# Recurrent stage of a two-block kernel: product groups coupled in the array's quarters, and the key norm placed inside a dense tile

## The chip, the cores and the metric

The kernel runs on one core of one Trainium2 chip. The metric is the device time of one execution in microseconds. Before the change it is 2938.91 us (median of 3 runs, 2938.07 to 2939.73).

## What is computed

The reference applies two blocks to 1024 tokens of width 1024. The change lies in the second block's RWKV-7 branch: 8 heads of 64 channels, with a state matrix that is carried from token to token.

```python
w = jnp.exp(-DECAY_SCALE * jax.nn.sigmoid(w_logit))       # w_logit = w0 + tanh(wd) @ w_decay_up
a = jax.nn.sigmoid((a0 + ad @ w_iclr_up))
kk = k * k_k
kk = kk / jnp.maximum(jnp.linalg.norm(kk, axis=-1, keepdims=True), 1e-12)
k = k * (1.0 + (a - 1.0) * k_a)
...
def step(S, inp):
    r_t, w_t, k_t, v_t, kk_t, a_t = inp
    sa = jnp.einsum('bhvk,bhk->bhv', S, -kk_t)
    S = S * w_t[:, :, None, :] + sa[..., None] * (kk_t * a_t)[:, :, None, :] + v_t[..., None] * k_t[:, :, None, :]
    return S, jnp.einsum('bhvk,bhk->bhv', S, r_t)
```

The output is normed per head, gained, given the term sum(r k r_k) v, gated and multiplied by a matrix.

## The kernel before, in words

The stage handles two heads at a time (a *pair*, four in all; pairs 1 and 2 are a loop), one head on partitions 0 to 63 and one on 64 to 127. A pair takes its 1024 tokens in two *halves* of 512, and a half is eight chunks of 64 tokens. Inside a half the recurrence is solved by products of 64x64 matrices: a matrix `lt` is built, its inverse is approached in five *levels* (per level a product `t`, then `x` and `xt`), and at the end the state is carried through the eight chunks (`ms0` to `ms7`).

**Product groups.** One group is one product for two heads and eight chunks, 16 matmuls of 64x64 (each shows as two records, so x32). A matmul of that size occupies one quarter of TensorE's array. `SAME` writes a head to its own partitions and `OTHER` to the other head's, so a `SAME` group uses two quarters and an `OTHER` group the two that are left. Where the code issues one of each in turn, chunk by chunk, this text calls it a *couple*; before, `lt` with `lt_x`, `l` with `kkp_tm`, `ke_tm` with `akv`, and `x` with `xt` are such.

**Filling.** TensorE also has dense tiles to do (48 matmuls of 128x512, each tile in one of two PSUM pairs `dps[:, 0]` and `dps[:, 1]`). `fill(n)` in `rw_half_pe` issues the next n of them between the product groups (line 300, `dense_part`), so that TensorE has work while VectorE and ScalarE take the products out of PSUM. A *slot* is `fill(n - 1)`, the waits, `fill(1)` and a group or couple. Ahead of level 1 a slot has 2 dense matmuls, in the levels 5. What is left of a half's tiles follows at its end. At the end of every tile GpSimd splits the next tile's weights into `w_hi` and `w_lo` (lines 2376 and 2378).

**Banks.** Products rotate over three PSUM banks (`bank`, `BANKS = 3`); `free(name)` waits until the product three places earlier in `PRODUCTS.names` has been taken, by a mask on VectorE (`VALUES`) or a copy on ScalarE (`COPIES`). A fourth bank, `k.aps[:, 3, :]`, holds the half's output `y`, and between, the previous half's `mean` and `var`.

**Engines' queues.** The order of each engine is written out by hand and is counted in semaphores. VectorE: `rw_half_dve` masks the products in order (line 1891), subtracts `x` and `xt` (line 1915), and between them does one step each of two other lists: `result_step` (the previous half's output: `centred`, four reciprocals `rstd`, `normed`, `gained`, `summed` at line 1972, and the gating) and `setup_step` (the coming half's `l`, `lp`, `rate`, `floor`, four reciprocals `unit`, `kk`, `b`, `k`). A pair's first half has both lists (the first pair's first half has only the setup), its second half only the result.

**Opening of a pair.** `rw_pair_pe`: two products for decay and learning rate into `dps[:, 0]` and `dps[:, 1]` (line 1536), the key norm (line 1541; it needs `rw_e`, the squared key, from ScalarE at line 2005, and that needs VectorE's token shift of the key at line 1762), then a dense tile for `v` and one for a gate. ScalarE (`rw_pair_act`): square, scaled copy, sigmoid of the decay (line 2009), sigmoid of the rate (line 2012), root of the norm (line 2014), exponentials. VectorE (`rw_pair_dve`): shifts of key and `r`, the setup steps, the eight products ahead of the half (`rw_ahead_dve`, the last is `rkv`), then it takes `v` out of `dps[:, 0]` and shifts it, which the half's first step (line 1895) needs.

## Time and profile before

| | |
|---|---|
| median of 3 runs | 2938.91 us |
| profiled execution | 2935.31 us |
| its span | 2933.5 us |
| TensorE busy | 2758.5 us (94%) |
| VectorE, GpSimd, ScalarE busy | 1374.6, 945.1, 682.8 us |
| mean granted TensorE clock | 0.98 |
| the recurrent stage, four pairs | from 2008.8 to about 2706 us of the span |

A shortening of TensorE's queue counts where no other engine is late. The rows tell it by stretch: busy time of an engine against the stretch, the wait in brackets ahead of a row, and what ended it. Matmul records overlap (each starts before the one ahead has ended), so the cost of one in a row of them is the distance between starts.

### The profile page before, as it was taken

What the parts mean: (1) busy time and instruction counts of PE and PEld (TensorE: products, weight loads), DVE (VectorE), ACT (ScalarE), POOL (GpSimd) and SP (SyncE); (2) the same over time, 40 slices, a digit from 0 to 9 for tenths busy, and PEclk for the clock granted to TensorE, in tenths of its full rate; (3) what the DMA queues carried; (4) which work ended last, traced back from release to release, by engine and by line L of the source; (5) the groups of instructions that cost most, each with busy time, mean ns of one, the idle gap of its engine ahead of it and who ended that gap; (6) DMA issues with size and microseconds to landing.
All of it is one profiled execution on the core that took longest, in us unless ns stands there. A gap on an engine that the chain in (4) does not pass through costs nothing. (4 is left out here: it accounts for less than half of the span.)

```text
span 2933.5 us, 48563 instructions
## 1 busy us (share of the span) xinstructions
PE 2758.5 (94%) x20356; PEld 2195.1 (75%) x20356; DVE 1374.6 (47%) x1332; ACT 682.8 (23%) x966; POOL 945.1 (32%) x417
## 2 busy tenths in 40 slices
PE   7999999999999999999998989989999999998886
PEld 6777778887888888888876767776767767676675
DVE  7844441124532122212565643345457465564589
ACT  3433330011211001000233234441222121222321
POOL 4222214443444444444533211103111121213365
PEclk9999999999999999999999999999999999998998
DMA  3100001112111111111121100001011111112343
GB/s 124 36 29 29 29 15 50 50 44 107 43 50 49 45 50 50 46 47 50 57 79 65 65 22 14 14 29 59 31 42 34 49 38 42 34 42 95 115 151 107
DMA packets 40746, 156.11 MB, mean 53 GB/s; under 512 B 4640, under 2 KB 5152, under 8 KB 39200
## 3 DMA queue, kind: packets, MB, share of 16 engines
q1 hardware_dynamic: 31392, 110.21, 11.4%
q10 hardware_dynamic: 9216, 43.78, 4.0%
q8 instruction: 121, 1.98, 0.3%
q14 instruction: 17, 0.14, 0.0%
HBM read 133.00 MB, written 20.97 MB: 52 GB/s over the span
## 5 line engine op out<-in xcount | busy, mean ns | idle before, releaser
L2376 POOL TENSOR_TENSOR w_hi<-w_raw,one 128x1024 fp32r<-128x1024 f32 x199 | 389.8, 1959 | 1931.9 <-PE dps L283 1500.4
L283 PE MATMUL dps<-h_hi,w_hi 128*128 128x512 f32 x1904 | 608.3, 395 | 46.0 <-issue 11.1
L283 PE MATMUL dps<-h_lo,w_hi 128*128 128x512 f32 x1904 | 602.2, 392 | 0.0
L283 PE MATMUL dps<-h_hi,w_lo 128*128 128x512 f32 x1904 | 600.2, 391 | 0.0
L2378 POOL TENSOR_TENSOR w_lo<-w_raw,w_hi 128x1024 fp32r<-128x1024 f32 x199 | 527.5, 2651 | 15.6
L283 PEld LDWEIGHTS dps<-h_hi,w_hi 128*128 128x128 f32 x1904 | 358.4, 190 | 134.8 <-issue 40.3
L283 PEld LDWEIGHTS dps<-h_lo,w_hi 128*128 128x128 f32 x1904 | 360.8, 190 | 75.8 <-issue 0.2
L283 PEld LDWEIGHTS dps<-h_hi,w_lo 128*128 128x128 f32 x1904 | 360.5, 189 | 76.1
L300 PE MATMUL dps<-h_hi,w_hi 128*128 128x512 f32 x352 | 128.8, 426 | 5.3 <-DVE rw_t L1891 5.3
L300 PE MATMUL dps<-h_lo,w_hi 128*128 128x512 f32 x352 | 129.5, 430 | 2.5 <-DVE rw_t L1891 1.6
L300 PE MATMUL dps<-h_hi,w_lo 128*128 128x512 f32 x352 | 121.7, 412 | 1.6 <-DVE rw_t L1891 1.6
L932 DVE TENSOR_TENSOR tmp<-dps,inv 128x1024 f32<-128x1024 f32 x22 | 26.9, 1225 | 204.6 <-PE dps L283 204.6
L283 PE MATMUL dps<-hid_hi,w_hi 128*128 128x512 f32 x352 | 108.4, 389 | 0.0
L283 PE MATMUL dps<-hid_lo,w_hi 128*128 128x512 f32 x352 | 108.4, 389 | 0.0
L283 PE MATMUL dps<-hid_hi,w_lo 128*128 128x512 f32 x352 | 108.4, 389 | 0.0
L946 DVE TENSOR_TENSOR x_res<-dps,x_res 128x1024 f32 x24 | 29.4, 1225 | 156.1 <-PE dps L283 156.1
L957 ACT ACTIVATE tmp<-tmp 128x1024 f32<-128x1024 f32 x22 | 23.3, 1061 | 336.9 <-DVE tmp L930 336.9
L678 DVE TENSOR_TENSOR_SCAN sb_f<-sb_f,zero 128x128 f32<-128x128 f32 (+7 forms) x64 | 88.1, 1377 | 19.1 <-ACT sb_f L735 18.9
L1269 PE MATMUL aps<-mla_k,mla_q 128*128 128x512 f32 (+2 forms) x192 | 81.3, 534 | 13.7 <-ACT mla_p L1410 9.0
L300 PEld LDWEIGHTS dps<-h_lo,w_hi 128*128 128x128 f32 x352 | 64.8, 188 | 29.0 <-issue 4.4
L784 DVE TENSOR_TENSOR tmp<-dps,inv 128x1024 f32<-128x1024 f32 x16 | 19.6, 1225 | 140.7 <-PE dps L283 140.7
L300 PEld LDWEIGHTS dps<-h_hi,w_hi 128*128 128x128 f32 x352 | 63.6, 187 | 28.5 <-DVE rw_t L1891 10.0
(355 smaller groups left out, 4218.7 us busy)
## 6 DMA issues: line engine op xcount, KB each, us to landing
w_raw<-w_stream SPq DMA_DIRECT2D x200, 512.0 KB, 3.3
x_again<-x_t ACTq DMA_DIRECT2D x2, 4096.0 KB, 13.0
gates<-gate_out ACTq DMA_DIRECT2D x16, 512.0 KB, 2.9
tmp<-gates ACTq DMA_DIRECT2D x16, 512.0 KB, 4.3
x_t<-x_res ACTq DMA_DIRECT2D x4, 1024.0 KB, 3.9
out_t<-x_again SPq DMA_DIRECT2D x16, 256.0 KB, 2.0
back<-branches ACTq DMA_DIRECT2D x7, 512.0 KB, 8.9
x_res<-x_t ACTq DMA_DIRECT2D x2, 1536.0 KB, 12.1
```

The costliest lines, as they stand in the source:

```text
L283: mm = k.nc.tensor.matmul(k.dps[0:rows, pair, h * HALF:(h + 1) * HALF], w[:, slot, sub + t, 0:rows], x(t)[:, h * HALF:(h + 1) * HALF], sta ...
L300: mm = k.nc.tensor.matmul(k.dps[:, pair, h * HALF:(h + 1) * HALF], w[:, slot, t, :], x[:, t, h * HALF:(h + 1) * HALF], start=n < 2, stop=n ...
L678: v.tensor_tensor_scan(back, back, k.zero[:, 0:1].to_broadcast([P, w]), 1.0, ALU.mult, ALU.add).then_inc(k.sem("sb_scan_done"), 1)
L784: v.tensor_tensor(k.tmp[g][:, :], k.dps[:, g, :], k.inv[:, :], ALU.mult).then_inc(k.sem(f"pair{g}_out"), 1)
L932: v.tensor_tensor(k.tmp1[:, :], k.dps[:, 1, :], k.inv[:, :], ALU.mult).then_inc(k.sem("pair1_out"), 1)
L946: v.tensor_tensor(one(k.x, n), k.dps[:, j, :], one(k.x, n), ALU.add).then_inc(k.sem(f"pair{j}_out"), 1)
L957: a.activation(k.tmp0[:, :], k.tmp0[:, :], ACT.Silu).then_inc(k.sem("silu_done"), 1)
L1269: mm = mul(k.aps[:, 2 * r + lo // HALF, 0:hi - lo], k.mla_q[:, b * P:(b + 1) * P], k.mla_k[:, lo:hi], start=True, stop=False, skip_group_c ...
L2376: g.tensor_tensor(k.w_hi[:, s], k.w_raw[:, s], ones, ALU.mult).then_inc(k.sem("w_hi_done"), 1)
L2378: g.tensor_tensor(k.w_lo[:, s], k.w_raw[:, s], k.w_hi[:, s].bitcast(F32), ALU.subtract).then_inc(k.sem("w_split"), 1)
```

## The change

In the diff `each`, `mul` and `turn` issue the 16 matmuls of a group. Lines cut are marked.

```diff
@@ -1436,11 +1436,13 @@
 
-PRODUCTS = Steps("rw_product", ["rk", "lt", "lt_x", "l", "kkp_tm", "ak_t", "rb_t", "rk_t", "v_tm", "be_tm", "ke_tm", "akv"]
-                 + LEVEL_NAMES + ["u0", "w1", "n", "m", "r"] + [f"ms{c}" for c in range(NC)])
-VALUES = Steps("rw_value", ["rkv", "lt", "xt_part", "xt0", "x_part", "x0", "ak_t", "rb_t", "rk_t"] + LEVEL_NAMES
-               + ["decay", "m", "r", "s_in"] + [f"s{c}" for c in range(NC)])
-COPIES = Steps("rw_copy", ["kkp_tm", "v_tm", "be_tm", "ke_tm", "akv", "u0", "w1", "n"])
+BESIDE = {"t2": "rk_t", "t3": "be_tm", "t4": "ke_tm"}
+LEVEL_PRODUCTS = [n for name in LEVEL_NAMES for n in (name, BESIDE.get(name)) if n is not None]
+PRODUCTS = Steps("rw_product", ["rk", "lt", "lt_x", "l", "kkp_tm", "ak_t", "v_tm", "akv", "rb_t"]
+                 + LEVEL_PRODUCTS + ["u0", "w1", "n", "m", "r"] + [f"ms{c}" for c in range(NC)])
+VALUES = Steps("rw_value", ["rkv", "lt", "xt_part", "xt0", "x_part", "x0", "ak_t", "rb_t"]
+               + [n for n in LEVEL_PRODUCTS if not n.endswith("_tm")] + ["decay", "m", "r", "s_in"] + [f"s{c}" for c in range(NC)])
+COPIES = Steps("rw_copy", ["kkp_tm", "v_tm", "akv", "be_tm", "ke_tm", "u0", "w1", "n"])
 
@@ -1448,6 +1450,7 @@
             **{n: (VALUES, n) for n in ["ak_t", "rb_t", "rk_t"] + LEVEL_NAMES + ["m", "r"]}, **{n: (COPIES, n) for n in COPIES.names}}
+ROTATING = [n for n in PRODUCTS.names if n not in BESIDE.values()]
 
@@ -1481,7 +1484,7 @@
 def bank(k, name):
-    return k.aps[:, PRODUCTS.names.index(name) % BANKS, :]
+    return k.aps[:, ROTATING.index(name) % BANKS if name in ROTATING else BANKS, :]
 
@@ -1530,17 +1533,19 @@
     pe.wait_ge(k.sem("rw_up_loaded"), i * 16 + 16)
-    for n, (use, done) in enumerate(((use0, "rw_w_done"), (use1, "rw_a_done"))):
-        pe.wait_ge(k.sem(f"pair{n}_out"), use + 2)
-        for h in range(2):
-            mm = mul(k.dps[:, n, h * HALF:(h + 1) * HALF], k.rw_up[HEADS[n], :], k.rw_wdad[HEADS[n], h * HALF:(h + 1) * HALF],
-                     start=True, stop=True)
-        mm.then_inc(k.sem(done), 1)
+    pe.wait_ge(k.sem("pair0_out"), use0 + 2)
+    pe.wait_ge(k.sem("pair1_out"), use1 + 2)
+    for h in range(2):
+        w, a = (mul(k.dps[:, n, h * HALF:(h + 1) * HALF], k.rw_up[HEADS[n], :], k.rw_wdad[HEADS[n], h * HALF:(h + 1) * HALF],
+                    start=True, stop=True) for n in range(2))
+    w.then_inc(k.sem("rw_w_done"), 1)
+    a.then_inc(k.sem("rw_a_done"), 1)
+    dense_part(k, pe, blk + 2, 0, 0, use0 + 2, "blk_done", 0, 3 * KT)
     pe.wait_ge(k.sem("rw_kk_sq_done"), i + 1)
...
     mm.then_inc(k.sem("rw_kk_norm_done"), 1)
-    dense(k, pe, blk + 2, 0, 0, rows(k.h_hi), rows(k.h_lo), KT, 0, use0 + 2, "blk_done")
+    dense_part(k, pe, blk + 2, 0, 0, use0 + 2, "blk_done", 3 * KT, 6 * KT)
     dense(k, pe, blk + 3, 1, 0, rows(k.h_hi), rows(k.h_lo), KT, 1, use1 + 2, "blk_done")
@@ -1572,7 +1577,7 @@
 
-        u.wait(pe, *TAKEN_BY[PRODUCTS.names[PRODUCTS.names.index(name) - BANKS]])
+        u.wait(pe, *TAKEN_BY[ROTATING[ROTATING.index(name) - BANKS]])
 
@@ -1631,39 +1636,44 @@
     free("ak_t")
+    free("v_tm")
     fill(1)
     each("ak_t", SAME, channel("kq"), channel("kkp"))
-    fill(FILL_MASKS - 1)
-    free("rb_t")
-    free("rk_t")
-    fill(1)
-    each("rb_t", SAME, channel("bq"), channel("rp"))
-    each("rk_t", SAME, channel("kq"), channel("rp"))
+    for c in range(NC):
+        mm = turn(bank(k, "v_tm"), SAME, c, value)
+    mm.then_inc(product, 1)
     if before is not None:
...
     fill(FILL_MASKS - 1)
-    free("v_tm")
-    free("be_tm")
-    fill(1)
-    for name, lhs in (("v_tm", value), ("be_tm", chunk("be"))):
-        for c in range(NC):
-            mm = turn(bank(k, name), SAME, c, lhs)
-        mm.then_inc(product, 1)
-    fill(FILL_MASKS - 1)
-    free("ke_tm")
     free("akv")
+    free("rb_t")
+    u.wait(pe, COPIES, "v_tm")
     fill(1)
     for c in range(NC):
-        a = turn(bank(k, "ke_tm"), SAME, c, chunk("ke"))
-        b = mul(bank(k, "akv"), OTHER, c, same("akt"), same("v_tm"))
+        a = mul(bank(k, "akv"), OTHER, c, same("akt"), same("v_tm"))
+        b = mul(bank(k, "rb_t"), SAME, c, channel("bq"), channel("rp"))
     a.then_inc(product, 1)
...
     for l in LEVEL_STEPS:
+        beside = BESIDE.get(f"t{l}")
         fill(FILL_T - 1)
...
         u.wait(pe, VALUES, "x0" if l == 1 else f"x{l - 1}")
+        if beside == "rk_t":
+            if before is not None:
+                before.wait(pe, Y_COPIES, "std")
+        elif beside is not None:
+            u.wait(pe, *TAKEN_BY[BESIDE[f"t{l - 1}"]])
         fill(1)
-        each(f"t{l}", OTHER, same("lt"), same("xm"))
+        for c in range(NC):
+            a = mul(bank(k, f"t{l}"), OTHER, c, same("lt"), same("xm"))
+            if beside == "rk_t":
+                b = mul(bank(k, "rk_t"), SAME, c, channel("kq"), channel("rp"))
+            elif beside is not None:
+                b = turn(bank(k, beside), SAME, c, chunk(beside[0:2]))
+        a.then_inc(product, 1)
+        if beside is not None:
+            b.then_inc(product, 1)
         fill(FILL_X - 1)
@@ -1683,9 +1693,7 @@
     u.wait(pe, VALUES, f"xt{LEVELS}")
-    u.wait(pe, COPIES, "akv")
-    if before is not None:
-        before.wait(pe, Y_COPIES, "std")
+    u.wait(pe, COPIES, "ke_tm")
     fill(1)
@@ -1901,14 +1909,18 @@
     result_step()
-    for name, out, which in (("ak_t", "akt", "strict_t"), ("rb_t", "arbt", "incl_t"), ("rk_t", "arkt", "incl_t")):
+    for name, out, which in (("ak_t", "akt", "strict_t"), ("rb_t", "arbt", "incl_t")):
         u.wait(dve, PRODUCTS, name)
...
         mask("t1", f"t{l}", f"lev{l}").then_inc(made, 1)
-        result_step()
+        if BESIDE.get(f"t{l}") == "rk_t":
+            u.wait(dve, PRODUCTS, "rk_t")
+            mask("arkt", "rk_t", "incl_t").then_inc(made, 1)
+        else:
+            result_step()
         for n, out in (("x", "xm"), ("xt", "xt")):
@@ -1983,6 +1995,7 @@
     a.activation(k.rw_wdad[0:HD, :], k.rw_wdad[0:HD, :], ACT.Tanh).then_inc(k.sem("rw_tanh_done"), 1)
+    rw_up_load(k, act, 0, w_up)
     rw_pair_act(k, act, 0, None, w_up, branches, gates)
@@ -1996,10 +2009,13 @@
 
+def rw_up_load(k, act, i, w_up):
+    act.dma_start(k.rw_up[:, :], w_up[bass.ds(i, 1)].rearrange("a p n -> p (a n)")).then_inc(k.sem("rw_up_loaded"), 16)
 def rw_pair_act(k, act, i, before, w_up, branches, gates):
...
     use0, use1 = i * RW_USES + (RW_USE0 + 1), i * RW_USES + RW_USE1
-    act.dma_start(k.rw_up[:, :], w_up[bass.ds(i, 1)].rearrange("a p n -> p (a n)")).then_inc(k.sem("rw_up_loaded"), 16)
     act.wait_ge(k.sem("rw_mix_done"), i * 3 + 2)
@@ -2010,6 +2026,8 @@
     a.activation(k.rw_b[:, :], k.dps[:, 1, :], ACT.Sigmoid, bias=vec(k, "a0", i)).then_inc(k.sem("pair1_out"), 1)
+    if not isinstance(i, int) or i < PAIRS - 1:
+        rw_up_load(k, act, i + 1, w_up)
     act.wait_ge(k.sem("rw_kk_norm_done"), i + 1)
@@ -2075,18 +2093,19 @@
         rw_result_act(k, act, before, "std")
-    copy("be_tm")
-    copy("ke_tm")
     copy("akv")
     if after is None:
-        for n in (2, 3):
-            rw_gate_act(k, act, u, n, gates)
-        if end:
-            back_load(k, act, u, branches, gates)
+        rw_gate_act(k, act, u, 2, gates)
     else:
...
         rw_exps_act(k, act, after)
+    copy("be_tm")
+    copy("ke_tm")
+    if after is None:
+        rw_gate_act(k, act, u, 3, gates)
+        if end:
+            back_load(k, act, u, branches, gates)
     copy("u0", -1.0)
```

The new order of a half's products: `ak_t` and `v_tm` one after the other in one slot; `akv` coupled with `rb_t`; `rk_t` coupled with `t2`, `be_tm` with `t3`, `ke_tm` with `t4`. The last three write the fourth bank. Two slots fewer stand ahead of level 1.

**TensorE, opening of the first pair.** Before, with `rw_e` the squared key and line 1536 the products for decay and rate:

```order
L283 MATMUL dps<-h_hi,w_lo 128x512 x2
L1536 MATMUL dps<-rw_wdad,rw_up 128x512 x4
L1541 MATMUL aps<-rw_e,const 128x512 x2
L283 MATMUL dps<-h_hi,w_hi 128x512 x2
L283 MATMUL dps<-h_lo,w_hi 128x512 x2
```

and with the change:

```order
L283 MATMUL dps<-h_hi,w_lo 128x512 x2
L1539 MATMUL dps<-rw_wdad,rw_up 128x512 x4
L300 MATMUL dps<-h_hi,w_hi 128x512 x2
L300 MATMUL dps<-h_lo,w_hi 128x512 x2
...
L300 MATMUL dps<-h_hi,w_lo 128x512 x2
L1546 MATMUL aps<-rw_e,const 128x512 x2
L300 MATMUL dps<-h_hi,w_hi 128x512 x2
```

The norm now has 24 dense matmuls of the `v` tile ahead of it and 24 behind.

**TensorE, first half, ahead of level 1.** Before (`rw_kq` stands in `ak_t` and `rk_t`, `rw_v`, `rw_be`, `rw_ke` in the groups that turn them into `v_tm`, `be_tm`, `ke_tm`, `rw_akt` in `akv`):

```order
L1581 MATMUL aps<-rw_kkp_154,rw_kq_158 64x64 x16
L300 MATMUL dps<-h_hi,w_hi 128x512 x2
L1581 MATMUL aps<-rw_rp_152,rw_bq_156 64x64 x16
L1581 MATMUL aps<-rw_rp_152,rw_kq_158 64x64 x16
L300 MATMUL dps<-h_lo,w_hi 128x512 x2
L1587 MATMUL aps<-const,rw_v 64x64 x16
L1587 MATMUL aps<-const,rw_be_160 64x64 x16
L300 MATMUL dps<-h_hi,w_lo 128x512 x2
L1587 MATMUL aps<-const,rw_ke_162 64x64 x2
L1581 MATMUL aps<-rw_v_tm,rw_akt 64x64 x2
```

and with the change, to the start of the couple in level 2:

```order
L1586 MATMUL aps<-rw_kkp_154,rw_kq_158 64x64 x16
L1592 MATMUL aps<-const,rw_v 64x64 x16
L300 MATMUL dps<-h_hi,w_hi 128x512 x2
L1586 MATMUL aps<-rw_v_tm,rw_akt 64x64 x2
L1586 MATMUL aps<-rw_rp_152,rw_bq_156 64x64 x2
...
L300 MATMUL dps<-h_hi,w_hi 128x512
L1586 MATMUL aps<-rw_xm,rw_lt 64x64 x16
...
L1586 MATMUL aps<-rw_xm,rw_lt 64x64 x2
L1586 MATMUL aps<-rw_rp_152,rw_kq_158 64x64 x2
```

Four slots have become two; rows in turn of x2 are couples.

**VectorE, first half, from the masks ahead of level 1 into level 2**, with the change:

```order
L1899 TENSOR_TENSOR rw_akt<-aps,const 128x512
L1899 TENSOR_TENSOR rw_arbt<-aps,const 128x512
L1816 SCALAR_TENSOR_TENSOR rw_l<-const,rw_sg 128x512
L1899 TENSOR_TENSOR rw_t_170<-aps,const 128x512
...
L1899 TENSOR_TENSOR rw_t_170<-aps,const 128x512
L1899 TENSOR_TENSOR rw_arkt<-aps,const 128x512
L1927 TENSOR_TENSOR rw_xm<-rw_xm,aps 128x512
```

Before, the mask `rw_arkt` stood directly behind `rw_arbt`; it is now behind the mask of `t2`.

## Rows read from the trace of the kernel before

**Rows 1.** The page's first part: busy us and share of the span of each engine.

```profile
PE 2758.5 (94%) x20356; PEld 2195.1 (75%) x20356; DVE 1374.6 (47%) x1332; ACT 682.8 (23%) x966; POOL 945.1 (32%) x417
```

**Rows 2.** Busy time by stretch, pair 1; columns: stretch, its us, then PE, PEld, DVE, ACT, POOL, granted clock, DMA.

```profile
2193.30:2216.50 23.20, 23.20 (x97) 19.06 (x97) 20.14 (x22) 7.01 (x9) 4.62 (x2) 0.94 0.07 23
...
2216.50:2289.60 73.10, 70.42 (x1272) 52.91 (x1271) 40.81 (x64) 16.94 (x23) 13.64 (x6) 1.00 0.12 42
...
2289.60:2360.00 70.40, 70.00 (x1271) 52.67 (x1269) 29.89 (x46) 9.51 (x14) 13.14 (x6) 1.00 0.13 45
```

**Rows 3.** Timeline of PE, pair 0, first half; columns: start, us, engine, line, operation, count.

```profile
2039.71 0.62 PE L283 MATMUL dps<-h_hi,w_lo 128*128 128x512 f32 x2
...
2042.43 0.62 PE L283 MATMUL dps<-h_hi,w_lo 128*128 128x512 f32 x2
...
2047.82 0.73 PE L300 MATMUL dps<-h_hi,w_lo 128*128 128x512 f32 x2
...
2049.56 0.73 PE L300 MATMUL dps<-h_hi,w_hi 128*128 128x512 f32 x2
...
2052.23 0.73 PE L300 MATMUL dps<-h_lo,w_hi 128*128 128x512 f32 x2
...
2054.91 0.73 PE L300 MATMUL dps<-h_hi,w_lo 128*128 128x512 f32 x2
...
2056.66 0.73 PE L300 MATMUL dps<-h_hi,w_hi 128*128 128x512 f32 x2
```

**Rows 4.** Timeline of PE, ACT and DVE, opening of pair 1.

```profile
2189.88 3.78 PE L1541 MATMUL aps<-rw_e,const 128*128 128x512 f32 x4 [4.45 <-ACT rw_e L2005]
...
2192.18 1.11 ACT L2009 ACTIVATE rw_sg<-dps,vec 128x1024 f32<-128x1024 f32 x1
...
2193.35 1.22 PE L283 MATMUL dps<-h_hi,w_hi 128*128 128x512 f32 x2
...
2194.36 1.05 PE L283 MATMUL dps<-h_lo,w_hi 128*128 128x512 f32 x2
...
2195.22 1.03 PE L283 MATMUL dps<-h_hi,w_lo 128*128 128x512 f32 x2
...
2195.62 1.03 ACT L2014 ACTIVATE rw_norm<-aps 128x1024 f32<-128x1024 f32 x1
...
2196.68 0.43 DVE L1817 TENSOR_SCALAR rw_norm<-rw_norm 128x512 f32<-128x512 f32 x1 [1.00 <-ACT rw_norm L2014]
...
2211.04 0.74 DVE L1863 SCALAR_TENSOR_TENSOR rw_rkv<-rw_r,vec,rw_k 128x512 f32<-128x512 f32 x1
...
2214.32 1.29 DVE L1762 SCALAR_TENSOR_TENSOR rw_v<-rw_d,vec,rw_v 128x1024 f32<-128x1024 f32 x1
```

**Rows 5.** Busy time by stretch: two restarts of PE (columns as in Rows 2).

```profile
2193.30:2196.10 2.80, 2.80 (x8) 2.17 (x8) 2.31 (x3) 2.77 (x3) 0.00 (x0) 0.50 0.00 0
...
1618.40:1622.60 4.20, 4.15 (x10) 3.31 (x11) 2.45 (x2) 1.65 (x2) 0.00 (x0) 0.50 0.00 0
```

**Rows 6.** Timeline of POOL and DVE, shift of the key, pair 1.

```profile
2184.25 3.20 POOL L2378 TENSOR_TENSOR w_lo<-w_raw,w_hi 128x1024 fp32r<-128x1024 f32 x1
...
2185.41 3.12 DVE L1762 SCALAR_TENSOR_TENSOR rw_k<-rw_d,vec,rw_k 128x1024 f32<-128x1024 f32 x1 [0.16 <-DVE rw_d L1760]
```

**Rows 7.** Timeline of DVE (pair 0) and of PE (pair 1), start of a half.

```profile
2048.00 0.68 DVE L1891 TENSOR_TENSOR rw_xm<-aps,const 128x512 f32<-128x512 f32 x1
...
2220.54 0.27 PE L1581 MATMUL aps<-rw_bq,rw_kkp 64*64 64x64 f32 x2
```

**Rows 8.** Timeline of POOL, DVE and PE, level 4 and 5.

```profile
2144.34 1.89 POOL L2376 TENSOR_TENSOR w_hi<-w_raw,one 128x1024 fp32r<-128x1024 f32 x1 [28.01 <-PE dps L300]
...
2144.42 2.36 DVE L1972 TENSOR_TENSOR rw_centred<-rw_centred,rw_rkv 128x512 f32<-128x512 f32 x1
...
2251.42 1.47 DVE L1972 TENSOR_TENSOR rw_centred<-rw_centred,rw_rkv 128x512 f32<-128x512 f32 x1
...
2258.05 0.49 PE L300 MATMUL dps<-h_hi,w_hi 128*128 128x512 f32 x1 [1.25 <-DVE rw_t L1891]
```

## The prediction

> **What bounds the kernel now.** I read the page first: TensorE is busy for 94% of the span [rows 1], so what shortens TensorE's own queue shortens the kernel, unless an engine that it waits for is late. Then the busy time by stage [rows 2]. The second half of a pair is TensorE alone (70.0 us busy of 70.4); the first half is 73.1 us long with 70.4 busy, so 2.7 us of it are waits, and the reader should see that VectorE is busy there for 40.8 us against 29.9. Then TensorE's timeline in a half, for the price of a product group [rows 3], and the timeline of a pair's opening, for the chain ahead of the half [rows 4]. There TensorE waits 4.45 us for the squared key, does the key norm in 3.5 us, and goes straight into the dense tile at 2193.35, which I call S below.
>
> **The product groups.** From the dense matmuls ahead of the `ak_t` slot to those ahead of `t1` it is 2056.66 - 2047.82 = 8.84 us [rows 3]: four slots with six group times and eight dense matmuls. The change leaves two slots. One holds two groups one after the other (`ak_t`, `v_tm`), as the slot from 2049.56 to 2052.23 does now: 2.67 us. One holds a couple (`akv` with `rb_t`), as the slot from 2054.91 to 2056.66: 1.75 us. `rk_t`, `be_tm` and `ke_tm` ride in `t2`, `t3`, `t4`; a couple there costs what a single group costs, since the `kq` group alone (2047.82 to 2049.56, 1.74 us with its two dense matmuls) is as long as the couple's slot. The four dense matmuls left out are done at the end of the half, 0.91 us at 0.227 each (twelve from 2039.71 to 2042.43). Sum: 8.84 - 2.67 - 1.75 - 0.91 = 3.51 saved in a half, **28.1 us** in eight. Bounds: no less than 2 x 0.93 us (2.67 - 1.74, a group time for each of `rk_t` and `be_tm`), and 4.42 where a half has no dense work to fill with (the very last).
>
> One new wait stands inside: `v_tm` takes the bank of `l`, so the `ak_t` slot now waits for the mask of `l`. That mask ran to 2048.68 [rows 7], while the second dense matmul of the slot started at about 2048.15. The wait costs about 0.45 us in each half, **+3.6 us**. Behind it are queued the rest of the slot and everything after it. `akv` now waits for the copy of `v_tm` soon after its product; the `var` product and one dense matmul cover that, except in the first half of all, which has no `var` product (half a us, in the range). The copies of `be_tm` and `ke_tm` move behind the exponentials or a gate copy on ScalarE; nothing needs them before levels 4 and 5, and ScalarE is busy for 17 of 73 us [rows 2], so I cost them at nothing. In level 2 the mask of `rk_t` (0.69 us) takes the place of one step of the result; cost nothing by itself.
>
> **The opening: TensorE's part.** The dense tile writes the bank that the decay product was in, so it starts when ScalarE's first sigmoid is done: 2192.18 + 1.11 = 2193.29, and the dense start is 2193.35 [rows 4]. The norm product ended at that same moment. The change does not touch ScalarE's order (square, scaled copy, sigmoid), so the tile cannot start earlier; taking the norm out of the wait frees nothing, and it costs its own time inside the tile. At the high clock its four passes take half of the 0.85 us that they take now, 1.7 us, with 0.1 around them: 1.8 us. Second, the wait is now empty: TensorE stands still for some 8 us before S, where the norm had half woken it. At S the granted clock is the low one (0.5) until 2196.10 today [rows 5]; after that it is the high one. From its first matmul at 2189.88 that is 6.2 us. At another restart, at 1618.4, it was low for 4.2 us. I take 5.1 us from S, between the two. A dense matmul takes 0.43 us at low clock (2194.36 to 2195.22 for two [rows 4]) and 0.227 at high, so each us at low clock loses 0.47. Against the 1.9 to 2.75 us at low clock that lie behind S today it is 2.7 us more on average: +1.25 us. A pair: 1.8 + 1.25 = 3.05, four pairs **+12.2 us**. Bounds for the clock part: 0.7 us (4.2) to 1.8 us (6.2) a pair. The decay and learning-rate products are interleaved; they end in front of the same wait, so they are worth nothing either way. The load of `rw_up` is issued from another place of ScalarE's queue, where it has time in hand.
>
> **The opening: VectorE's part.** The norm now ends after 24 dense matmuls, S + 5.1 + 12.4 x 0.227 + 1.8 = S + 9.7. With the root (1.03 us) and the hand-overs VectorE takes `floor` at S + 10.95 instead of S + 3.33 (2196.68) [rows 4]: 7.6 us later. From there it is 15.1 us of its own work to the end of `rkv` at 2211.78, so S + 26.05, and I add 0.35 because more of it now falls beside GpSimd: S + 26.4. TensorE is ready for the `rk` product at S + 26.0. So far nothing is lost. But VectorE then takes `v` and shifts it, and the `rkv` of the half and the mask of `lt` queue behind that. Today `v` is ready at 2215.61, 0.9 us before `rk` at 2216.5. In the new order the take begins just as the second tile ends, and that is when GpSimd splits the next weights. What this does stands at the shift of `k`, in the same position [rows 6]: its second operation took 3.12 us and ended 1.1 us after GpSimd's, where that of `v` today, with GpSimd idle, takes 1.29 [rows 4]; the operation ahead of it was lengthened as well. I take the dear values: `v` is ready at S + 32.4, the mask of `lt` ends at S + 33.8, the `l` group starts at S + 34.3. TensorE alone would be there at today's S + 27.2 [rows 7] + 3.0 = S + 30.2. Loss 4.1 us a pair, **+16.4 us**. Bounds: the cheap values take 2.0 us off a pair; a low clock of 4.2 or 6.2 us moves it by 0.4.
>
> **The levels.** A half now has eight dense matmuls before level 1 and ten in a level, so the 48th, which ends a tile and lets GpSimd split weights, moves from before the `x4` slot into it. GpSimd then works from about 0.25 to 4.7 us after the slot's start, and VectorE's next operation on two SBUF inputs starts some 2.4 us after it: `summed` where a result is computed, `kk` in the first half of all. Such an operation waited for GpSimd's to end and ended 0.55 us behind it: `summed` took 2.36 us beside a split of 1.89, and 1.47 where the meeting was shorter [rows 8]. It would now end 5.25 us after the slot's start, with the mask of `t5` behind it, and in first halves a reciprocal and `kk` as well. Against the waits of today (1.25 us at that mask in a first half, part of the 2.7 [rows 2, 8]) I get 2.1 us more in the three first halves that carry both, 1.3 in the very first, 0.6 in second halves: 6.3 + 1.3 + 2.4 = **+10.0 us**. Bounds: nothing (the meeting falls elsewhere) to 15.
>
> **Sum.** -28.1 + 3.6 + 12.2 + 16.4 + 10.0 = +14.1 us, against the profiled execution of 2935.3 us: 2949.4. The median of the runs shown is 3.6 us above that execution, so 2953.0 us. A measurement of this kernel can tell 0.2% (5.9 us) from no change: below 2933.0 is faster, above 2944.8 slower.
>
> **The rivals.** (a) *VectorE catches up* (faster, 0.14): the key norm's delay is absorbed, the `l` group starts when TensorE gets there and the levels meet no split. Then only TensorE's own terms count: -28.1 + 3.6 + 12.2 = -12.3, so 2926.6. For it: VectorE is idle for 3 us of the 23 behind S [rows 2]. Against: `v` has only 0.9 us in hand and gets 7.6 us of delay less the 3 that TensorE loses too. It decides where the `v` shift ends: before S + 28.
>
> (b) *Half of the meetings with GpSimd do not happen* (no change, 0.18): cheap shift (-8.0) or cheap levels (-10.0), or both: +6 to -4, 2935 to 2945.
>
> (c) *The products leave PSUM too slowly* (slower, 0.04): rows 2 show VectorE busy for 40.8 of 73.1 us in a first half, and more products now come at once. If the extra mask in level 2 held up every half by its 0.69 us, that is 5.5 more: 2958.5. The Trainium skill, TensorEngine Tiling (Array Packing), Performance Considerations, says that tiling speeds up TensorE but not the evacuation of PSUM, which can then be the bottleneck. By that rule the couples would be worth less than their slots; the rows bear it out in first halves only.
>
> (d) *The couples do not overlap* (slower, 0.04): each of the three new couples in a level costs a second group, about 1.0 us: 3 x 8 = 24 more, 2977. Against it stand the equal slots of rows 3.
>
> **How the numbers follow.** The forecast itself has 0.60: 2946 to 2963, from the clock's bounds (4 us either way over four pairs) and the levels' (5 up). With (c) and (d) slower has 0.68, (b) gives same 0.18, (a) faster 0.14. The range for 8 in 10 leaves out (a) and (d) and takes in (b): 2934 to 2963.
>
> **What would show it.** Right: `t2` to `t4` slots no longer than today; the dense tile's start still on the first sigmoid; VectorE's `v` shift at over 4 us beside a split; the granted clock low for 4 to 6 us behind each dense start; second halves near 68 us (70.4 - 3.5 + 0.45 + 0.6), first halves near 76 (73.1 + 4.1 - 3.5 + 0.45 + 2.1). Wrong: the `l` group starting without a wait, or first halves that shrink as the second ones do; then (a) holds. A dense start before the sigmoid's end would overturn the opening's whole term.

## The result, and the profile after

The changed kernel takes 2957.03 us (median of 4 runs, 2956.03 to 2957.95), the kernel before 2938.49 (4 runs, 2937.75 to 2939.73). The ratio is 1.0059, with a 95% interval of 1.0044 to 1.0075: slower by 18.5 us. The profiled execution took 2957.55 us, its span is 2955.8, its mean granted clock 0.974.

The page's first part, the counterpart of [rows 1]. TensorE is busy for 18 us less than before, in a span that is 22 us longer; the change did take work out of TensorE's queue, and waits grew by more.

```profile
PE 2740.1 (93%) x20356; PEld 2182.3 (74%) x20356; DVE 1381.6 (47%) x1332; ACT 685.1 (23%) x966; POOL 946.5 (32%) x417
```

Busy time by stretch of pair 1, columns as in [rows 2]: from the dense start to the half, the first half, the second half.

```profile
2201.97:2228.71 26.74, 26.36 (x101) 20.60 (x101) 17.03 (x20) 6.96 (x9) 4.86 (x3) 0.90 0.06 20
...
2228.70:2305.80 77.10, 69.36 (x1271) 51.57 (x1272) 46.69 (x67) 17.27 (x23) 13.46 (x6) 0.98 0.11 40
...
2305.80:2373.60 67.80, 66.40 (x1271) 50.05 (x1269) 29.27 (x46) 9.83 (x14) 12.82 (x6) 1.00 0.13 45
```

The second half went from 70.4 to 67.8 us, the first from 73.1 to 77.1, although TensorE is busy for 1.1 us less in it; the stretch ahead went from 23.2 to 26.7. The waits of TensorE name the engines (columns: who waited for what, us in total, times, longest).

```profile
PE dps L300 <- ACT rw_sg L2025: 31.3, 4, 7.9
PE dps L300 <- DVE rw_t L1899: 16.0, 16, 2.6
PE dps L300 <- DVE rw_lt L1899: 14.0, 4, 4.1
```

The wait for the first sigmoid is the old standstill in front of the norm, which the norm no longer interrupts. The one for the mask of `lt` is new, and that for the masks of `t` was 8.6 us before, 15 times.

The opening of pair 1 in the timeline of PE, ACT, DVE and POOL; it answers to [rows 4, 6].

```profile
2200.80 1.11 ACT L2025 ACTIVATE rw_sg<-dps,vec 128x1024 f32<-128x1024 f32 x1
...
2201.97 1.22 PE L300 MATMUL dps<-h_hi,w_hi 128*128 128x512 f32 x2 [7.90 <-ACT rw_sg L2025]
...
2210.08 1.88 PE L1546 MATMUL aps<-rw_e,const 128*128 128x512 f32 x4
2211.39 1.03 PE L300 MATMUL dps<-h_hi,w_hi 128*128 128x512 f32 x2
...
2213.05 0.43 DVE L1825 TENSOR_SCALAR rw_norm<-rw_norm 128x512 f32<-128x512 f32 x1 [8.75 <-ACT rw_norm L2032]
...
2227.91 0.75 DVE L1871 SCALAR_TENSOR_TENSOR rw_rkv<-rw_r,vec,rw_k 128x512 f32<-128x512 f32 x1
2228.57 1.22 DVE L1780 TENSOR_TENSOR rw_v<-dps,inv 128x1024 f32<-128x1024 f32 x1
2229.82 1.66 DVE L1768 TENSOR_TENSOR rw_d<-rw_v 128x1024 f32<-128x1024 f32 x1
2231.63 3.15 DVE L1770 SCALAR_TENSOR_TENSOR rw_v<-rw_d,vec,rw_v 128x1024 f32<-128x1024 f32 x1
...
2228.47 1.93 POOL L2395 TENSOR_TENSOR w_hi<-w_raw,one 128x1024 fp32r<-128x1024 f32 x1 [6.25 <-PE dps L283]
2230.48 3.21 POOL L2397 TENSOR_TENSOR w_lo<-w_raw,w_hi 128x1024 fp32r<-128x1024 f32 x1
...
2236.26 0.50 PE L300 MATMUL dps<-h_lo,w_hi 128*128 128x512 f32 x1 [3.31 <-DVE rw_lt L1899]
2236.69 0.28 PE L1586 MATMUL aps<-rw_bq,rw_kkp 64*64 64x64 f32 x2
```

The reader should see three things. The dense tile starts 0.06 us behind the end of the first sigmoid, as before. VectorE stands still for 8.75 us until the root of the norm is there. Its chain then reaches `v` 0.1 us after GpSimd's first operation has begun, the last operation of the shift takes 3.15 us where 1.29 was enough before [rows 4], and the `l` group starts at S + 34.72.

Level 5 of the same half, timeline of DVE, POOL and PE: `summed` (line 1984) takes 2.64 us beside the split, and the dense matmul that follows the mask of `t5` waits for 2.55 us.

```profile
2264.72 1.89 POOL L2395 TENSOR_TENSOR w_hi<-w_raw,one 128x1024 fp32r<-128x1024 f32 x1 [31.02 <-PE dps L300]
2266.69 2.37 POOL L2397 TENSOR_TENSOR w_lo<-w_raw,w_hi 128x1024 fp32r<-128x1024 f32 x1
...
2266.96 2.64 DVE L1984 TENSOR_TENSOR rw_centred<-rw_centred,rw_rkv 128x512 f32<-128x512 f32 x1
...
2271.85 0.50 PE L300 MATMUL dps<-h_lo,w_hi 128*128 128x512 f32 x1 [2.55 <-DVE rw_t L1899]
```

And what the prediction did not have. Stretches behind standstills (columns as in [rows 2], the last but two is the granted clock): behind the dense start; from the `l` group to `t1` in the first halves of pairs 0, 1, 2 and 3; and behind the level-5 wait.

```profile
2201.97:2207.40 5.43, 5.43 (x13) 4.32 (x14) 2.29 (x3) 2.23 (x2) 0.00 (x0) 0.50 0.00 0
...
2056.04:2066.91 10.87, 10.65 (x202) 8.22 (x201) 3.75 (x6) 1.79 (x3) 0.00 (x0) 0.63 0.11 44
2236.69:2245.03 8.34, 7.99 (x204) 5.91 (x204) 4.67 (x8) 4.93 (x7) 0.00 (x0) 1.00 0.18 67
2418.75:2428.18 9.43, 9.39 (x205) 6.86 (x204) 4.66 (x8) 4.94 (x7) 0.00 (x0) 0.82 0.16 59
2602.36:2613.38 11.02, 10.89 (x204) 8.00 (x203) 4.60 (x8) 4.30 (x6) 0.00 (x0) 0.69 0.13 50
...
2272.25:2275.66 3.41, 3.41 (x37) 2.98 (x37) 1.50 (x4) 0.00 (x0) 0.00 (x0) 0.50 0.00 0
```

Behind most of the new waits inside a half TensorE's clock is at its lower level (0.50, which is 1.2 GHz) for a while. The same slots take 8.34 us at the full clock and 9.43 to 11.02 where part of them runs at the low one.

**The stage in a sum.** With the starts of the same matmuls in the timeline as marks (tile end, dense start, `rk`, `l`, `t1`, `u0`), and sums over the four pairs:

| stretch | before | after | difference |
|---|---|---|---|
| start of the stage | 2008.7 | 2009.8 | +1.1 |
| dense start to `rk` | 91.8 | 105.2 | +13.5 |
| `rk` to `l`, first halves | 15.9 | 32.3 | +16.3 |
| `l` to `t1`, first halves | 47.7 | 39.7 | -8.0 |
| `l` to `t1`, second halves | 48.6 | 33.5 | -15.1 |
| `t1` to `u0`, first halves | 109.6 | 118.9 | +9.3 |
| `t1` to `u0`, second halves (three) | 76.3 | 77.8 | +1.5 |
| `u0` to the end of a half (seven) | 200.7 | 207.5 | +6.8 |
| last `t1` to the end of the stage | 45.8 | 45.6 | -0.2 |
| behind the stage | 226.8 | 223.9 | -2.9 |

The tile end to the dense start (11.36 us a pair) and `rk` to `l` of second halves (4.03) are the same in both.

### The profile page after: what moved, and what is told of

It reads as the page before. It is cut to its first block and busy times, and to the rows that moved or that the text cites. A ratio compares the mean times of both kernels' runs of the same rounds, so it can differ in the third digit from the quotient of the medians.

```text
span 2955.8 us, 48554 instructions
## 1 busy us (share of the span) xinstructions
PE 2740.1 (93%) x20356; PEld 2182.3 (74%) x20356; DVE 1381.6 (47%) x1332; ACT 685.1 (23%) x966; POOL 946.5 (32%) x417
## 5 line engine op out<-in xcount | busy, mean ns | idle before, releaser
L283 PE MATMUL dps<-h_hi,w_lo 128*128 128x512 f32 x1840 | 580.7, 391 | 0.0
L2397 POOL TENSOR_TENSOR w_lo<-w_raw,w_hi 128x1024 fp32r<-128x1024 f32 x199 | 531.2, 2669 | 15.6
L283 PEld LDWEIGHTS dps<-h_hi,w_lo 128*128 128x128 f32 x1840 | 348.0, 189 | 73.0
L300 PE MATMUL dps<-h_hi,w_lo 128*128 128x512 f32 x416 | 151.6, 428 | 4.2 <-DVE rw_t L1899 2.0
L932 DVE TENSOR_TENSOR tmp<-dps,inv 128x1024 f32<-128x1024 f32 x22 | 26.9, 1225 | 204.6 <-PE dps L283 204.6
L300 PEld LDWEIGHTS dps<-h_hi,w_lo 128*128 128x128 f32 x416 | 80.0, 195 | 30.7 <-DVE rw_xm L1899 5.2
```

Source lines behind the costliest of these rows:

```text
L283: mm = k.nc.tensor.matmul(k.dps[0:rows, pair, h * HALF:(h + 1) * HALF], w[:, slot, sub + t, 0:rows], x(t)[:, h * HALF:(h + 1) * HALF], sta ...
L300: mm = k.nc.tensor.matmul(k.dps[:, pair, h * HALF:(h + 1) * HALF], w[:, slot, t, :], x[:, t, h * HALF:(h + 1) * HALF], start=n < 2, stop=n ...
L932: v.tensor_tensor(k.tmp1[:, :], k.dps[:, 1, :], k.inv[:, :], ALU.mult).then_inc(k.sem("pair1_out"), 1)
L2397: g.tensor_tensor(k.w_lo[:, s], k.w_raw[:, s], k.w_hi[:, s].bitcast(F32), ALU.subtract).then_inc(k.sem("w_split"), 1)
```

## The experiments

The first theory in the texts below is the prediction's: fewer slots shorten TensorE's queue, but the later norm carries VectorE's `v` shift into GpSimd's split. Ratios are to the kernel before in the same job, whose median was 2939.2 us for the first four kernels and 2937.6 for the others.

### The groups without the opening

```diff
-    dense_part(k, pe, blk + 2, 0, 0, use0 + 2, "blk_done", 0, 3 * KT)
...
-    dense_part(k, pe, blk + 2, 0, 0, use0 + 2, "blk_done", 3 * KT, 6 * KT)
+    dense(k, pe, blk + 2, 0, 0, rows(k.h_hi), rows(k.h_lo), KT, 0, use0 + 2, "blk_done")
```

The products for decay and rate stand one after the other again, as before.

> The changed kernel with the pair's opening put back (products for decay and rate one after the other, the key norm ahead of the dense tile). Theory 1 (the opening costs about 30 us: 13.5 in TensorE's own queue and 16 in the wait for VectorE at the l group; the groups are a gain, given back in part by VectorE meeting GpSimd in the levels): 2926 us, 12 us under the kernel before; second halves 2.2 us shorter than before, first halves of pairs 1 to 3 about as long as before. Theory 2 (products cannot be taken from PSUM fast enough, the groups are the loss): 2938 or more. Theory 3 (the opening costs only TensorE's own 12 us, the rest of the loss lies in the groups): 2945.

Measured: 2919.88 us (6 runs), ratio 0.9938 (0.9926 to 0.9951): 19.4 us faster than before, 37 faster than the whole change. Its waits for the masks of `t`, for the mask of `l` (written to `rw_xm`), and for that of `lt`:

```profile
PE dps L300 <- DVE rw_t L1897: 15.3, 16, 2.6
PE dps L300 <- DVE rw_xm L1897: 3.2, 8, 0.5
...
PE dps L300 <- DVE rw_lt L1897: 0.4, 1, 0.4
```

The wait for `lt` is gone (0.4 us once, as before), that for the masks of `t` stays: the one belongs to the opening, the other to the groups. `l` to `t1` takes 33.3 us in the four first halves, against 47.7 before and 39.7 with the whole change; without the `lt` wait there is no low clock there. The gain is above the expected one, and about 3 us of that lie behind the recurrent stage, where this kernel needs 223.6 us.

### The norm inside the tile, on the kernel before

```diff
+    dense_part(k, pe, blk + 2, 0, 0, use0 + 2, "blk_done", 0, 3 * KT)
     pe.wait_ge(k.sem("rw_kk_sq_done"), i + 1)
...
-    dense(k, pe, blk + 2, 0, 0, rows(k.h_hi), rows(k.h_lo), KT, 0, use0 + 2, "blk_done")
+    dense_part(k, pe, blk + 2, 0, 0, use0 + 2, "blk_done", 3 * KT, 6 * KT)
```

> The kernel before with one edit: the key norm issued after the first 24 dense matmuls of the v tile. Theory 1: 30 us above the kernel before, 2968; the stretch from the dense start to the rk product 3.3 us longer in each pair and from there to the l group 4.0 us longer. Theory 3: 12 to 13 us above, 2951, with nothing between rk and l. Theory 2: 18 us above at most, 2957.

Measured: 2981.59 us (4 runs), ratio 1.0146 (1.0131 to 1.0161): 42.4 us slower. The two terms that were foreseen measure +14.5 (dense start to `rk`) and +16.6 (`rk` to `l`), as in the whole change. The rest is 5.4 us of low clock behind the `lt` wait (the last stretch of this view) and 4.7 us behind the stage; the four make 41.2 us, and the spans differ by 40.5.

```profile
2202.51:2229.53 27.02, 26.64 (x100) 20.80 (x100) 17.02 (x20) 6.96 (x9) 4.85 (x3) 0.89 0.06 20
2237.81:2251.10 13.29, 13.29 (x301) 10.63 (x301) 5.74 (x8) 4.17 (x7) 0.00 (x0) 0.82 0.10 39
```

The parts alone sum to -19.4 + 42.4 = +23.0 us; together they give +18.5. So they hardly act on each other, and the opening alone makes the change slower.

### The norm after 6 dense matmuls instead of 24

```diff
-    dense_part(k, pe, blk + 2, 0, 0, use0 + 2, "blk_done", 0, 3 * KT)
+    dense_part(k, pe, blk + 2, 0, 0, use0 + 2, "blk_done", 0, 6)
...
-    dense_part(k, pe, blk + 2, 0, 0, use0 + 2, "blk_done", 3 * KT, 6 * KT)
+    dense_part(k, pe, blk + 2, 0, 0, use0 + 2, "blk_done", 6, 6 * KT)
```

> The changed kernel with the key norm after 6 dense matmuls of the tile and not after 24; TensorE's work is the same. Theory 1: the norm is ready some 5.5 us sooner, v is shifted before GpSimd begins to split, and the wait at the l group goes (4.0 us a pair) with the low clock that follows it: 2932 us. Theory 3 (only TensorE's own time counts): unchanged, 2957. If VectorE's lateness counts but not GpSimd: the wait shrinks to nothing as well, so this run tells theory 1 from 3 and not GpSimd's part.

Measured: 2934.51 us (12 runs), ratio 0.9987 (0.9978 to 0.9995): 22.5 us below the changed kernel. In the timeline of pair 1 the last operation of the `v` shift ends before GpSimd's split begins:

```profile
2219.53 1.29 DVE L1770 SCALAR_TENSOR_TENSOR rw_v<-rw_d,vec,rw_v 128x1024 f32<-128x1024 f32 x1
...
2221.56 1.89 POOL L2395 TENSOR_TENSOR w_hi<-w_raw,one 128x1024 fp32r<-128x1024 f32 x1 [5.78 <-PE dps L283]
```

`rk` to `l` is 15.9 us over four pairs, exactly the value of before, and `l` to `t1` is 33.3. The dense start to `rk` keeps 104.0 of its 105.2 us, since the norm still costs its time and the clock is still low behind the dense start. So 22.7 us of the change (16.3 of wait and 6.4 of low clock behind it) hang on when VectorE gets to the `v` shift.

### Twelve dense matmuls ahead of level 1 again, on the groups alone

```diff
-FILL_MASKS, FILL_T, FILL_X, FILL_N, FILL_M, FILL_S = 2, 5, 5, 5, 6, 2
+FILL_MASKS, FILL_T, FILL_X, FILL_N, FILL_M, FILL_S = 3, 5, 5, 5, 6, 2
```

The opening is that of the kernel before. With three in a slot instead of two, the four slots ahead of level 1 hold twelve, as the six did before, so a tile ends, and GpSimd splits, at the place in the levels where it did before.

> As e1_groups_only, with three dense matmuls in each of the four slots ahead of level 1 and not two, so that the 48th dense matmul and GpSimd's split come at the same place of level 4 as before the change. Theory 1: the meeting of VectorE and GpSimd in level 4 is as before, and the wait for the mask of l is covered: 12 to 14 us below e1_groups_only, 2912 to 2914 us. If the longer levels come from the masks of the coupled products and not from GpSimd: 3.6 us below e1_groups_only (the mask's wait alone), about 2922.

Measured: 2902.86 us (5 runs), ratio 0.9886 (0.9869 to 0.9903): 17.0 us below the groups alone. `t1` to `u0` of the four first halves is 109.1 us (before 109.6, groups alone 118.8). The wait for the masks of `t`, and pair 1 by stretch (first half, second half):

```profile
PE dps L300 <- DVE rw_t L1897: 6.6, 12, 1.2
```

Columns as in [rows 2]:

```profile
2209.55:2279.20 69.65, 67.28 (x1272) 50.13 (x1271) 39.86 (x64) 17.27 (x23) 13.36 (x6) 1.00 0.12 44
2279.20:2346.00 66.80, 66.61 (x1271) 49.94 (x1269) 29.47 (x46) 9.72 (x14) 12.88 (x6) 1.00 0.13 46
```

The longest of these waits falls from 2.6 to 1.2 us, and the clock is 1.00 in both halves. The groups and their masks are the same in both kernels, so it is the place of the dense matmuls that lengthened the levels. In pair 1 `summed` takes 0.83 us now, against 1.47 before and 2.64 with the change: its step of the result has moved back by the mask of `rk_t`, while the split is back from 19.7 to 17.8 us behind the start of `t1`, where it was before. The second halves gain another us (67.85 to 66.80), the waits for the mask of `l` are 0.8 us in four against 3.2 in eight, and some 3 of the 17 us lie behind the stage (220.8 against 223.6).

### The norm after the whole tile

```diff
-    dense_part(k, pe, blk + 2, 0, 0, use0 + 2, "blk_done", 0, 3 * KT)
+    dense(k, pe, blk + 2, 0, 0, rows(k.h_hi), rows(k.h_lo), KT, 0, use0 + 2, "blk_done")
...
-    dense_part(k, pe, blk + 2, 0, 0, use0 + 2, "blk_done", 3 * KT, 6 * KT)
```

> The changed kernel with the key norm behind the whole v tile (48 dense matmuls, 5.4 us later than in the change). If VectorE's operations on two SBUF inputs wait for GpSimd's splits to end: the two that met the first split (3.9 us lost) now come after it, and most of the shift of v after the second; the l group starts only 0.5 us later than in the change, the time is 2959 us. If the lateness alone counts and GpSimd does not: 5.4 us more in each pair, 2979 us.

Measured: 2968.76 us (4 runs), ratio 1.0104 (1.0089 to 1.0120), between the two expectations. The timeline of DVE and POOL tells why:

```profile
2230.42 1.60 DVE L1847 TENSOR_TENSOR rw_be<-rw_b,rw_t 128x512 f32<-128x512 f32 x1 [0.69 <-ACT rw_t L2057]
2231.95 2.82 DVE L1847 TENSOR_TENSOR rw_ke<-rw_k,rw_t 128x512 f32<-128x512 f32 x1
...
2237.98 1.29 DVE L1769 SCALAR_TENSOR_TENSOR rw_v<-rw_d,vec,rw_v 128x1024 f32<-128x1024 f32 x1
...
2229.08 2.40 POOL L2394 TENSOR_TENSOR w_hi<-w_raw,one 128x1024 fp32r<-128x1024 f32 x1 [8.33 <-PE dps L283]
2231.56 2.67 POOL L2396 TENSOR_TENSOR w_lo<-w_raw,w_hi 128x1024 fp32r<-128x1024 f32 x1
```

The `v` shift is clear of the second split, at its 1.29 us, and the products `be` and `ke` meet it: 1.60 and 2.82 us where one takes 0.69. That by itself is no new loss. In the changed kernel two other operations of the chain, `b` and `k` of the setup, take 2.31 and 2.88 us beside the first split, and here these are clear of it. From `floor` to the end of `rkv` VectorE needs 15.1 us before, 15.6 with the change and 16.3 here (where `floor` meets the end of the first split, last section). What decides is that the norm comes later still: `floor` starts at S + 16.19 instead of S + 11.08, and the shorter `v` shift gives only part of that back. So the `l` group starts at S + 38.3, and over the pairs 3.5 to 5.7 us later than in the changed kernel. The wait moved from `lt` to `rk` (26.1 us in four, by the page's waits), and `rk` to `l` runs partly at the low clock (25.2 us for 15.9).

### A standstill filled with idle matmuls

```diff
     a.then_inc(k.sem("rw_a_done"), 1)
+    for _ in range(32):
+        mul(k.aps[:, 2, :], k.h_hi[:, 0, 0:P], k.h_hi[:, 0, 0:HALF], start=True, stop=True)
```

On the whole change, into a bank that nobody reads, to see what the low clock behind the dense start costs.

> The changed kernel with 32 matmuls of 128x512 added behind the products for decay and rate, into a bank that nobody reads; they fill TensorE's standstill ahead of the dense tile and change no result. If the low clock behind the standstill is a cost of the change: the granted clock stays high, the first 24 dense matmuls take 5.4 us and not 8.1, norm and rk come 2.7 us sooner, 2957 - 11 = 2946 us. If the clock is no part of it: 2957 us or, should the added matmuls end late, more.

Measured: 2956.56 us (4 runs), ratio 1.0061 (1.0045 to 1.0076): no gain. The granted clock behind the dense start is 1.00, and from a tile's end to `rk` it is 2.1 us less a pair (142.3 against 150.7 over four). But the `lt` wait is unchanged (14.0 us), and now the clock also falls behind it in pair 1, where it stayed at 1.00 in the changed kernel (first row: from the dense start; second: from the `l` group):

```profile
2199.79:2205.00 5.21, 5.21 (x23) 4.31 (x24) 2.30 (x3) 2.24 (x2) 0.00 (x0) 1.00 0.00 0
...
2232.29:2242.00 9.71, 9.65 (x222) 7.32 (x223) 4.95 (x7) 5.47 (x7) 0.00 (x0) 0.86 0.14 53
```

`l` to `t1` is 2.3 us longer, the ends of second halves 2.2, the part behind the stage 3.6: together they return what the opening gained. The price of the low clock at one place is measured by this; that it can be saved as a whole is not.

### The sigmoids ahead of the square on ScalarE

```diff
-    act.wait_ge(k.sem("rw_mix_done"), i * 3 + 2)
-    fixed_wait(k, act)
-    a.activation(k.rw_e[:, :], k.rw_k, ACT.Square, scale=vec(k, "k_k", i)).then_inc(k.sem("rw_kk_sq_done"), 1)
-    a.activation(k.rw_kk[:, :], k.rw_k, ACT.Copy, scale=vec(k, "k_k", i)).then_inc(k.sem("rw_kk_done"), 1)
     act.wait_ge(k.sem("rw_w_done"), i + 1)
...
     a.activation(k.rw_b[:, :], k.dps[:, 1, :], ACT.Sigmoid, bias=vec(k, "a0", i)).then_inc(k.sem("pair1_out"), 1)
+    act.wait_ge(k.sem("rw_mix_done"), i * 3 + 2)
...
```

The prediction said that taking the norm out of the wait frees nothing, because the tile waits for the sigmoid and the sigmoid stands behind the square. Here the sigmoid no longer does.

> The changed kernel with one edit on ScalarE: in a pair's opening both sigmoids stand ahead of the square and the scaled copy of the key. Theory 1 (the dense tile is held by the first sigmoid, which stands behind the square, and that behind VectorE's shift of the key): the tile starts 6.7 us sooner, 4.7 us behind the end of the k tile, at the high clock; norm, VectorE's chain and the l group follow 9.5 us sooner than in the change: 2957 - 38 = 2919 us. If the tile was held by something else: 2957 us.

Measured: 2928.79 us (6 runs), ratio 0.9970 (0.9957 to 0.9982): 28 us below the changed kernel. From the tile's end to the dense start it is 4.9 to 6.0 us a pair instead of 11.36. The dense start of pair 1 is at 2188.07, behind this in the timeline of ACT:

```profile
2185.61 1.28 ACT L2021 ACT_TABLE_LOAD   x1 [15.47 <-PE dps L1539]
2186.91 1.11 ACT L2021 ACTIVATE rw_sg<-dps,vec 128x1024 f32<-128x1024 f32 x1
```

The gain is 10 us below the expected one. In pairs 1 and 2 ScalarE loads the sigmoid's table only when the product is there, and its 1.28 us are on the path: the tile starts 6.0 us behind the tile's end, against 4.9 in pairs 0 and 3, where no load stands ahead of the first sigmoid. Both are more than the expected 4.7, together 3 us. From the dense start to `rk` 7.3 us are gained in four pairs where 11 were expected. The `lt` wait (14.0 us) is that of the changed kernel, and `l` to `t1` behind it takes 41.5 us, against 39.7 there.

### Sigmoids first, norm after 12, twelve dense matmuls ahead of level 1

Three edits of the changed kernel together: the sigmoids first, `FILL_MASKS` 3, and the norm earlier, here with 12 dense matmuls ahead of it, a place that was not run by itself.

> All that the runs so far pay for: sigmoids first, the key norm after 12 dense matmuls, three dense matmuls in each slot ahead of level 1. Theory 1: e4_groups_fill_12 (2903 us) less 6.4 us a pair, because the tile starts 6.7 us sooner, the norm ends 2 us sooner than in the kernel before and v is shifted in time: 2877 us. If VectorE's chain from the norm to rkv is the bound and does not get shorter: 2 us a pair below e4, 2895 us.

Measured: 2892.12 us (5 runs), ratio 0.9845 (0.9832 to 0.9859), 45 us below the kernel before and the fastest of all. Pair 1 by stretch (dense start to half, first half), and the last operation of its `v` shift beside GpSimd's first operation:

```profile
2177.27:2202.52 25.25, 25.25 (x101) 20.03 (x101) 22.23 (x24) 9.04 (x11) 4.62 (x2) 0.93 0.14 45
2202.52:2273.32 70.80, 68.37 (x1272) 50.51 (x1270) 43.47 (x66) 17.28 (x23) 14.23 (x6) 1.00 0.12 43
```

```profile
2202.92 2.88 DVE L1770 SCALAR_TENSOR_TENSOR rw_v<-rw_d,vec,rw_v 128x1024 f32<-128x1024 f32 x1
...
2202.83 1.90 POOL L2395 TENSOR_TENSOR w_hi<-w_raw,one 128x1024 fp32r<-128x1024 f32 x1 [6.25 <-PE dps L283]
```

The shift starts a tenth of a us behind GpSimd in this pair and so still pays 1.5 to 1.6 us in each pair: the first half is 1.15 us longer than with twelve dense matmuls and the old opening. The time is 3 us below the expectation for a chain of VectorE that bounds.

## Why the prediction was right, and where its sum was off

The direction, the range (2934 to 2963) and the likeliest case hold. The profiled execution came out 8.1 us above the sum of 2949.4, the median 4.0 above 2953.0. The 4.0 flatters the sum, since the profiled execution of before lay 3.2 us below the median that the result gives for it, and that of after 0.5 above. The sum is of spans, and there it is 8.2 us short; the range was wide enough for that. Term by term:

| term | forecast | measured |
|---|---|---|
| product groups, with the wait for the mask of `l` | -24.5 | -22.9 |
| opening, TensorE's part | +12.2 | +13.5 |
| opening, VectorE's part | +16.4 | +16.3 |
| levels meeting GpSimd | +10.0 | +10.8 |
| low clock behind the `lt` wait | none | +6.4 |
| ahead of and behind the stage | none | -1.8 |
| sum | +14.1 | +22.3 (the spans: 2955.8 - 2933.5) |

The measured values come from the table of stretches. For the groups I take `l` to `t1` of the groups alone (33.3, all at the full clock) and of the second halves: 33.3 + 33.5 - 96.3 = -29.5, and add 6.8 for the dense matmuls at the ends of halves and -0.2 for the last. The 6.4 are the difference of 39.7 to those 33.3.

**The groups.** Right, to 1.6 us. The couples in the levels cost no time of their own (last section). The waits for the mask of `l` are 3.2 us in eight in the groups alone (1.9 in five with the whole change, where the `lt` wait hides most of those in first halves), forecast 3.6. Rivals (c) and (d) fall: second halves, with three couples each, became 2.6 us shorter. Rival (b) falls too: both meetings with GpSimd took place, at 3.15 us for the shift and 2.64 for `summed`.

**TensorE's part of the opening.** Right in the main. The dense tile still starts on the first sigmoid, and the experiment that moved the sigmoid moved the tile by 5.3 to 6.5 us. The clock is low for 5.28, 5.43, 3.29 and 4.45 us behind S in the four pairs (forecast 5.1; pair 2 falls out of the 4 to 6 us that were named as a sign), the norm takes 1.31 us of the queue (2210.08 to 2211.39) and the dense matmul behind it 0.4 more, together near the 1.8. Of the 13.5 us, 1.4 are not TensorE's: `rk` waits for `rkv` for some 0.4 us in each pair. The prediction has that gap in its working, `rkv` done at S + 26.4 against TensorE ready at S + 26.0, and calls it nothing lost. With the norm after 6 it is gone.

**VectorE's part.** The chain came out within half a us at every step: `floor` at S + 11.08 (10.95), `rkv` done at S + 26.7 (26.4), `v` ready at S + 32.8 (32.4), the `l` group at S + 34.7 (34.3). The norm after 6 took all of it away. Of the 4.1 us a pair, 2.3 are the meeting with the split, read from the two lengthened operations (1.66 against 1.23 us with the norm after 6, and 3.15 against 1.29); the rest is VectorE's lateness itself. Meetings with the first split are hardly a part of it: they lengthened VectorE's chain by 3.3 us before (`be` and `ke`) and by 3.8 after (`b` and `k`), and it is 15.6 us long, forecast 15.45. The share of 2.3 is read, not tried: the norm after 6 removed both, and no run removed one alone. Rival (a) fell on the point that it named, the end of the `v` shift before S + 28.

**The levels.** Right in total. The mechanism is shown by the run with twelve dense matmuls, which took away 9.7 us of first halves. But its size is made up otherwise: in pair 1 the wait behind `t5` grew by 1.3 us (2.55 against 1.25 [rows 8]), and the 3.41 us at half the clock hold 1.7 us of lost work, an estimate. They can cost less on the path: in the run with the sigmoids first the same wait (2.58 us) stands in pair 2 and the clock stays at 1.00 behind it, and `t1` to `u0` takes 29.7 us there, against 30.8 in pair 2 of the changed kernel. That is 1.1 us, measured. The first halves of pairs 1 to 3 pay 2.5 to 3.0 us, forecast 2.1; a second half 0.5, forecast 0.6.

**The step that failed** is one that the prediction did not make: it asked for the clock only at the opening, where TensorE restarts anyway, and costed a wait inside a half at its own length. Three of the four `lt` waits and all three waits behind `t5` in the first halves of pairs 1 to 3 were also followed by work at the low clock. That is the +6.4, and 3 to 5 us of the 10.8 that the levels cost (three times 1.1 to 1.7), where waits shorter than forecast made up for it, which is luck. With the 6.4 the sum would have been 20.5, not 14.1. It also shows in the halves: the first ones of pairs 1 to 3 took 77.1, 78.2 and 79.5 us where the prediction named 76, the second ones 68.0 as named.

**Left open.** The part behind the recurrent stage, whose code is the same in all kernels, took 226.8 us before, 223.9 with the change, 231.5 with the norm alone, 227.4 with the norm after the whole tile and 220.8 with twelve dense matmuls. TensorE waits there for VectorE (10.2 us in five before, 6.4 in four after). I did not try what decides it; it is why no sum over the stage is better than some 3 us, and 5 where the norm alone is concerned.

## What to carry to other kernels

When a step is moved later on a path that another engine has in hand, ask not only how much slack there is but which of that engine's operations will now stand beside a neighbour's. Here a norm 24 matmuls later ran VectorE out of slack and into GpSimd's split, 22.7 us with what followed; with 6 matmuls ahead of it instead none of that was left. Cost a new wait of the length met here (2.6 to 4.1 us) with the low clock behind it, which followed six of the seven in first halves, and if slots are taken out ahead of a place that was tuned, give the work between back (here one dense matmul more in each remaining slot, worth 17 us) so that everything behind keeps its place.

## What the runs showed of the hardware

**A short standstill lowers TensorE's clock, and not always.** The `lt` waits of the first halves (4.1 us in pair 0, 3.3 in the others) were followed by a lower clock in pairs 0, 2 and 3, and that of 2.55 us in level 5 by 3.41 us at 0.50. The `lt` wait of pair 1 was not (1.00), and with the standstill of the opening filled it was (0.86 over the stretch behind it). With the norm alone it is pair 2 that keeps the full clock behind the same 3.30 us. So length alone does not decide it, and no run here tells what else does.

**VectorE beside GpSimd.** `v` is taken from PSUM with one input in SBUF: 1.22 us beside the split, 1.21 alone. The shift behind it with two inputs in SBUF took 3.15 instead of 1.29. At the first split of a pair it was `be` and `ke` that met GpSimd in the kernel before (1.81 and 2.88 us, 0.69 alone), `b` and `k` in the changed one (2.31 and 2.88). With the norm after the whole tile even `floor`, which has one input in SBUF, took 1.93 instead of 0.43:

```profile
2219.10 1.93 DVE L1824 TENSOR_SCALAR rw_norm<-rw_norm 128x512 f32<-128x512 f32 x1 [13.86 <-ACT rw_norm L2031]
...
2218.34 2.40 POOL L2396 TENSOR_TENSOR w_lo<-w_raw,w_hi 128x1024 fp32r<-128x1024 f32 x1
```

It ended 0.29 us behind `w_lo`. The Trainium skill, SBUF — State Buffer, Who interferes with whom, says that the shared port pair is an exclusive lock, that a VectorE operation with two SBUF inputs contends with a GpSimd operation that reads SBUF, and that tensor_scalar can contend too, in its two-port modes. The traces agree in the first two cases; for `floor` they fit, but no trace tells in which mode it ran.

**Couples cost what single groups cost.** From `t2` to `t3` in the second half of pair 1 it is 4.90 us with `rk_t` in `t2` (2323.18 to 2328.08), and 4.89 with `t2` alone before (2310.75 to 2315.64).
